# Four transformer blocks on one core: the boundaries between the stages, split finer and covered by one more row panel

## The reference

```python
h = x
for layer in range(2):
    y = rmsnorm(h, norm_g[layer, 0])
    y = gmlp_mixer(y, ...) if layer == 0 else diff_attention(y, ...)
    h = h + rmsnorm(y, norm_g[layer, 1])
    y = rmsnorm(h, norm_g[layer, 2])
    y = conv_ffn(y, ...)                 # (gelu(conv(y @ gate)) * conv(y @ up)) @ down, d_ff = 2816
    h = h + rmsnorm(y, norm_g[layer, 3])
x = h
x = x + 0.5 * swiglu(rms_norm(x, ffn1_norm), ...)
u = rms_norm(x, mix_norm) @ w_in
x = x + concat(mla_attention(u, ...), moba_attention(u, ...)) @ w_out
x = x + 0.5 * swiglu(rms_norm(x, ffn2_norm), ...)
return rms_norm(x, final_norm)
```

## Time and profile before

| | |
|---|---|
| median of three runs | 1125.63 us (1125.15 to 1126.83) |
| the profiled execution | 1125.67 us, span of its trace 1123.9 us |
| TensorE busy | 1079.8 us, 96% of the span |
| VectorE, ScalarE, GpSimd busy | 734.1, 606.5 and 37.8 us |
| granted TensorE clock, mean | 0.99 |

### The profile page before, as it was taken

How to read it: one execution, slowest core, us unless ns; L and a number is a source line. 1 busy time by engine, 2 the same in 40 slices (tenths; PEclk the granted TensorE clock), 3 DMA queues, 4 the chain that set the end, 5 groups by cost and what they waited for, 6 DMA issues and landing times.

```text
span 1123.9 us, 17895 instructions
## 1 busy us (share of the span) xinstructions
PE 1079.8 (96%) x7236; PEld 987.2 (88%) x7236; DVE 734.1 (65%) x1145; ACT 606.5 (54%) x1060; POOL 37.8 (3%) x39
## 2 busy tenths in 40 slices
PE   6999999999899789999999999999999989999997
PEld 4887999998799669999997999999899978999996
DVE  4887877666768667867667654455666846545543
ACT  5566665556655656655557543444455646344333
POOL 0640000000000000000000000000000000000000
PEclk9999999999999899999999999999999989999999
DMA  9664785565464225765563755555353514655541
GB/s 346 199 209 155 206 246 179 190 198 171 150 225 130 77 75 179 264 194 172 189 199 100 261 177 196 190 171 195 127 174 122 187 57 158 213 193 171 193 162 38
DMA packets 56257, 197.76 MB, mean 176 GB/s; under 512 B 6560, under 2 KB 8008, under 8 KB 56176
## 3 DMA queue, kind: packets, MB, share of 16 engines
q1 hardware_dynamic: 55920, 196.42, 53.8%
q0 software_dynamic: 112, 0.20, 0.1%
q10 hardware_dynamic: 144, 0.00, 0.0%
HBM read 195.35 MB, written 1.25 MB: 175 GB/s over the span
## 4 chain that ended last, share of the span: by engine, by line
PE 89%; DVE 5%; ACT 4%; issue 1%; DMA 0%; DVEq 0%; SPq 0%; ACTq 0%
PE Y L1260 25%; PE G L1225 16%; PE G L1227 16%; PE G L1226 16%; PE G L1248 3%; PE G L1249 3%; PE G L1250 3%; DVE w_low L744 1%; PE Y L1268 1%; PE Y L1226 1%; PE Y L1225 1%; PE Y L1227 1%; PE G L1378 1%; ACT big L431 1%; ACT L406 1%
## 5 line engine op out<-in xcount | busy, mean ns | idle before, releaser
L744 DVE TENSOR_TENSOR w_low<-raw,w_high 128x1024 fp32r<-128x1024 f32 x352 | 428.1, 1225 | 60.4 <-ACT w_high L399 59.0
L1225 PE MATMUL G<-x_parts,w_high 128*128 128x256 f32 x1504 | 426.6, 284 | 0.0
L1227 PE MATMUL G<-x_parts,w_low 128*128 128x256 f32 x1504 | 425.5, 283 | 0.0
L1226 PE MATMUL G<-x_parts,w_high 128*128 128x256 f32 x1504 | 425.5, 283 | 0.0
L399 ACT CAST w_high<-raw 128x1024 fp32r<-128x1024 f32 x352 | 359.5, 1046 | 11.5 <-DMA raw<-in_panels 7.8
L1225 PEld LDWEIGHTS G<-x_parts,w_high 128*128 128x128 f32 x1504 | 288.3, 192 | 3.4 <-DVE qk L875 0.3
L1226 PEld LDWEIGHTS G<-x_parts,w_high 128*128 128x128 f32 x1504 | 288.3, 192 | 2.7
L1227 PEld LDWEIGHTS G<-x_parts,w_low 128*128 128x128 f32 x1504 | 288.3, 192 | 0.0
L1260 PE MATMUL Y<-w_high,a_high 128*128 128x512 f32 x448 | 141.6, 398 | 3.9 <-DVE a_low L1057 2.0
L1260 PE MATMUL Y<-w_high,a_low 128*128 128x512 f32 x448 | 139.9, 393 | 0.0
L1260 PE MATMUL Y<-w_low,a_high 128*128 128x512 f32 x448 | 138.9, 391 | 0.0
(11 more groups left out here) (208 smaller groups left out, 935.2 us busy)
## 6 DMA issues: line engine op xcount, KB each, us to landing
raw<-in_panels SPq DMA_DIRECT2D x352, 512.0 KB, 4.5
gain_pre<-in_gains SPq DMA_DIRECT2D x7, 512.0 KB, 5.5
gain_post<-in_gains SPq DMA_DIRECT2D x4, 512.0 KB, 7.7
big<-in_xT SPq DMA_DIRECT2D x4, 256.0 KB, 8.0
h<-in_x SPq DMA_DIRECT2D x2, 512.0 KB, 8.7
big<-rel_rows SPq DMA_DIRECT2D x8, 128.0 KB, 6.1
out_y<-w SPq DMA_DIRECT2D x4, 256.0 KB, 2.0
big<-in_w_s SPq DMA_DIRECT2D x1, 512.0 KB, 10.1
```

The lines of the kernel that those rows point to most:

```text
L744: v.tensor_tensor(WL[:, n % RING, :], raw[:, n % RAWS, :], WH[:, n % RING, :].bitcast(F32), ALU.subtract).then_inc(lo, 1)
L1225: mm(out, WH[:, j, c:c + w], xh, start=first, stop=False, skip_group_check=skip)
L1226: mm(out, WH[:, j, c:c + w], xl, start=False, stop=False, skip_group_check=skip)
L1227: return mm(out, WL[:, j, c:c + w], xh, start=False, stop=last, skip_group_check=skip)
```

## The change

- `tail` takes the boundary's number and any number of row panels. The FFNs keep six row panels back for it instead of five (`_ffn_order`, `FFN_ORDER[4:-6]`); the two mixers' and the attention's tails keep five. `rows` for the last panel now goes by column halves: three matmuls for c = 0, then three for c = 1, each with its own signal (`y_there`).
- The transposes of the first token half's first four tiles are issued by `tail` itself: behind the last part (boundaries 1 and 3) or ahead of it (2, 4, 5 and 6: `early`).
- The normed stream, its transposes and its high and low parts are made in three pieces of 2, 2 and 4 tiles (`PARTS`) instead of two of 4; the third piece of t = 0 is turned into a bank of G. The transposes of t = 1 stand behind all matmuls of t = 0.
- The low parts of panels base + 3 and base + 4 are made by GpSimd (`BY_POOL`, `low_parts`), twelve panels in all; DVE leaves them out. ACT makes base + 4 within the boundary, before it reads the transposes.
- On DVE the gained copy of c = 0 comes first, and at boundaries 1 to 4 the third low part of t = 0 stands in the middle of the work on t = 1.
- Start: panel 6 is loaded ahead of x; ACT and DVE make panel 7 before the first and panel 8 before the second half of x's squares; PE computes the t = 1 products of panels 4 to 7 before it spreads the inverse roots (`r0_ps`), and DVE copies those (`rkvs`) after the first statistics instead of before them.
- End: `final_norm` multiplies h by the gain while ACT squares it, and scales one column half on ACT and the other on DVE.

```diff
+BY_POOL = [STARTS[b] + i for b in range(1, 7) for i in (3, 4)]
+PARTS = ((0, 2), (2, 2), (4, 4))
...
-        if 4 <= f < NF - 1:
+        if 4 <= f < NF - 2:
             seq.append(("d", f - 4))
-    return seq + [("d", f) for f in range(NF - 5, NF)]
+    return seq + [("d", f) for f in range(NF - 6, NF)]
...
# SyncE
-                    sp.wait_ge(lo, n - RAWS + 1)
+                    sp.wait_ge(*low_made(n - RAWS))
...
-            load(5)
+            load(5), load(6)
             for t in range(TT):
                 sp.dma_start(h[:, t, :], io["x"][t]).then_inc(x_in[t], 16)
-            load(6)
...
# GpSimd
+            def low_parts(b):
+                for n in BY_POOL[2 * (b - 1):2 * b]:
+                    pool.wait_ge(hi, n + 1)
+                    g.tensor_tensor(WL[:, n % RING, :], raw[:, n % RAWS, :], WH[:, n % RING, :].bitcast(F32),
+                                    ALU.subtract).then_inc(lo_pool, 1)
...
# ScalarE, boundary
                 if b in POST:
                     y_square(b, 0, 0), y_square(b, 0, 1)
                     y_root(b, 0)
                     upto(base + 3)
                 h_rms(b, 0)
-                if b < 7:
-                    x_high(b, 0, 0)
+                upto(base + 4)
+                x_high(b, 0, 0), x_high(b, 0, 1)
                 if b in POST:
                     y_square(b, 1, 0)
-                if b < 7:
-                    x_high(b, 0, 1)
+                x_high(b, 0, 2)
...
+            def final_norm():
+                for t in range(TT):
+                    h_rms(7, t)
+                    act.wait_ge(hg_r, 2 * t + 1)
+                    act.wait_ge(rs7_r, t + 1)
+                    s.activation(xn[:, t, half(0)], xn[:, t, half(0)], ACT.Copy, scale=rs2[:, t:t + 1])\
+                        .then_inc(out0_r, 1)
...
-            upto(6)
+            upto(7)
             h_rms(0, 0)
+            upto(8)
             h_rms(0, 1)
...
# VectorE, boundary
                 if b in POST:
-                    y_gained(b, 0, 1)
                     y_gained(b, 0, 0)
                     y_half_mean(b, 0)
+                    y_gained(b, 0, 1)
                     h_add(b, 0)
-                    half_mean(b, 0)
-                    upto(base + 3)
-                    x_normed(b, 0)
...
+                half_mean(b, 0)
+                x_normed(b, 0)
+                x_low(b, 0, 0), x_low(b, 0, 1)
+                if b in POST:
+                    y_gained(b, 1, 0)
+                    y_half_mean(b, 1)
+                    x_low(b, 0, 2)
+                    y_gained(b, 1, 1)
+                    h_add(b, 1)
                 else:
+                    x_low(b, 0, 2)
                     h_plus_y(b, 1)
...
+            def final_norm():
+                dve.wait_ge(gn_in, 16 * 7)
+                for t in range(TT):
+                    h_plus_y(7, t)
+                    dve.wait_ge(h_r, quarter(7, t, 1))
+                    for c in range(2):
+                        v.tensor_tensor(xn[:, t, half(c)], h[:, t, half(c)], gN[:, half(c)], ALU.mult).then_inc(hg_r, 1)
+                    half_mean(7, t)
+                    dve.wait_ge(h_std, 14 + t + 1)
+                    v.reciprocal(rs2[:, t:t + 1], sd2[:, t:t + 1]).then_inc(rs7_r, 1)
...
# TensorE, rows and tail
+                if last:
+                    for c in range(2):
+                        for x, w, start, stop in three:
+                            end = mm(Y[:, 2 * t + c, :], x, w[:, j, half(c)], start=start, stop=stop)
+                        end.then_inc(used if t == 1 and c == 1 else y_done, 1)
+                    return
...
-                for i in range(4):
+                for i in range(last):
                     part(i, 0)
                 part(0, 1)
-                part(4, 0).then_inc(y_done, 1)
-                for i in range(1, 4):
+                part(last, 0)
+                for i in range(1, last):
                     part(i, 1)
-                part(4, 1)
+                if early:
+                    turn_x(b, 0, 0), turn_x(b, 0, 1)
+                part(last, 1)
+                if b < 7:
+                    if not early:
+                        turn_x(b, 0, 0), turn_x(b, 0, 1)
+                    turn_x(b, 0, 2)
...
             value_panels(0, 4, (0,)).then_inc(v_ps, 1)
+            value_panels(0, 4, (1,))
             pe.wait_ge(rs0_r, 1)
...
             last.then_inc(r0_ps, 1)
-            value_panels(0, 4, (1,))
```

More of the change, by code:

```diff
@@ L251, in seen_turns, with low_made, y_there, sixth @@
             return a if a < HEADS else HEADS + 2 * (a - HEADS) + m
+        def low_made(n):
+            if n in BY_POOL:
+                return lo_pool, BY_POOL.index(n) + 1
+            return lo, n + 1 - sum(m < n for m in BY_POOL)
+        def y_there(b, t, c):
+            if t == 1 and c == 1:
+                return used, STARTS[b]
+            return y_done, 3 * (b - 1) + 2 * t + c + 1
+        def sixth(b, t, i):
+            return 6 * (b - 1) + 3 * t + i + 1
         def quarter(b, t, c):
@@ L381, in _ @@
             g.tensor_copy(bias[:, :, 0:P], bias[:, :, SC - P:SC]).then_inc(bias_r, 1)
+            for b in range(2, 6):
+                low_parts(b)
             pool.wait_ge(kr_r, 1)
@@ L436, in h_rms, with x_high @@
                     .then_inc(h_std, 1)
-            def x_high(b, t, c):
-                act.wait_ge(xt_r, quarter(b, t, c))
-                s.copy(x_half(0, t, c), y_half(t, c)).then_inc(xh_r, 1)
+            def x_high(b, t, i):
+                act.wait_ge(xt_r, sixth(b, t, i))
+                s.copy(x_rows(0, t, i), turned(t, i)).then_inc(xh_r, 1)
             def boundary(b, func):
@@ L730, in _ @@
             ffn(3, FFN3, False)
-            boundary(7, None)
+            final_norm()
         @block.vector
@@ L1212, in _ @@
             ffn(3, FFN3, False)
-            boundary(7)
+            final_norm()
         @block.tensor
@@ L1242, in values @@
                     if b:
-                        pe.wait_ge(xl_r, quarter(b, t, k // 4))
+                        pe.wait_ge(xl_r, sixth(b, t, min(k // 2, 2)))
                     else:
@@ L1257, in rows @@
                 xh, xl = AH[:, slot, tok(t)], AL[:, slot, tok(t)]
-                for x, w, start, stop in ((xh, WH, first, False), (xl, WH, False, False), (xh, WL, False, last)):
+                three = ((xh, WH, first, False), (xl, WH, False, False), (xh, WL, False, last))
+                if last:
[4 more added lines that the diff above has]
+                    return
+                for x, w, start, stop in three:
                     for c in range(2):
@@ L1300, in first_four @@
                     last.then_inc(done, 1)
-                turn_x(b, 1, 1)
+                for i in range(3):
+                    turn_x(b, 1, i)
                 for p in range(4):
@@ L1347, in ffn @@
                         tile_out(n, out(f, 0 if kind == "g" else 1))
-                last = range(NF - 5, NF)
-                tail(base + 3 * NF, [f % KT for f in last],
+                last = range(NF - 6, NF)
+                tail(b + 1, [f % KT for f in last], b < 6,
                      {(i, 0): (lambda f=f: hidden_seen(f)) for i, f in enumerate(last)})
@@ L1498, in _ @@
             head_rows(2, 1)
-            tail(FFN1, range(3, HEADS),
+            tail(3, range(3, HEADS), False,
                  {(0, 0): lambda: head_split(3),
@@ L1639, in _ @@
             weigh_values(15, 1)
-            tail(FFN3, [(k + 4) % KT for k in range(3, 8)],
+            tail(6, [(k + 4) % KT for k in range(3, 8)], True,
                  {(0, 0): lambda: out_split(3),
```

141 lines of the change are left out of this document (63 added, 78 removed).

## The result

The changed kernel took 1129.2 us (median of 11 runs, 1127.8 to 1133.2) against 1125.9 us for the kernel before in the same session: ratio 1.0025, 95% interval 1.0014 to 1.0035. So it is slower, by some 2.8 us, where 10.3 us of gain were forecast. Executions of one and the same kernel differ: the kernel before ran for 1125.1 to 1130.2 us, at mean granted clocks of 0.990 to 0.982, so a single trace shows one of several patterns of low clock.

The account below looks back on a forecast made before the run. TensorE, busy 1079.8 of 1123.9 us, was taken as the bound. Boundaries (2 x 1.35 + 0.3 + 1.8 + 0.85 + 0.75), start 4.3 and end 0.8 make 11.5, less 1.2 contention: 10.3 off 1125.7, 1115.4 us; range 1112.3 to 1119.8.

Parts of the forecast that it names:

- the contention: At the six boundaries, GpSimd's panels slow DVE by 0.2 us each, 1.2 us in all.
- (d): Rival: at boundaries GpSimd and DVE shut each other out on two SBUF inputs; up to 34 us, 1148 us; chance 0.05.
- twelve low panels ran beside GpSimd and eleven kept their time: Argument from the old trace's DVE rows against mutual shutting out: one low panel took 1.76 us instead of 1.22.
- GpSimd's own length: A 1024-column low panel takes GpSimd 2.8 us at the least, 7.1 at the most; its length costs nothing.
- The start: Before the first row sums: panel 7 ready earlier, so PE reaches them at 34.35 instead of 39.06; gain 4.3 us.
- Rival (b): At the start, late panel 7 or 9 or `rkvs` leaves only 1.3 of 4.3 us: 1118.4 us; chance 0.13.
- The boundaries: Earlier first t = 1 matmul: 1.35 us each at 1 and 3, 0.3 at 2, 1.8 at 4, 0.85 at 5, 0.75 at 6.
- rival (c): The clock stays up at boundary 2 and DVE is not disturbed: gain 12.7 us, 1113.0 us; chance 0.15.
- The wait of 2.8 us at boundary 2: PE waits 2.8 us before the first transposes, a clock drop is counted behind it, leaving 0.3 us gain.
- Rival (e): Split pieces and signals cost their savings; with another clock drop at boundary 4 and the start's loss, 1125 us; chance 0.03.
- In between PE runs through: Between the start, the boundaries and the end PE has no idle time, so no other edit can win there.
- The end: Behind the last matmul, the normed stream ends at E + 3.25 instead of E + 4.05, the store unchanged; gain 0.8 us.

Follow-up runs that it names:

- the fourth experiment: Changed kernel with GpSimd's two-input subtraction replaced by a one-input multiplication at the same places (result not the reference's): ratio 0.9904, 1115.1 us.
- the first experiment: Changed kernel with GpSimd's twelve low panels given back to DVE, all else kept: ratio 0.9907, 1115.4 us.
- the eighth experiment: Changed kernel with DVE making GpSimd's panels, lambdas' exponential behind boundary 2, final half mean between the gain multiplications, c = 1 stored first: ratio 0.9865, 1110.7 us.
- fifth: Changed kernel with each of GpSimd's twelve low panels made by four instructions of 256 columns instead of one of 1024: ratio 0.9938, 1118.9 us.
- ninth: Changed kernel with DVE's normed stream reading one SBUF input, the gain left out at boundaries 1 to 6 (another result): ratio 1.0028.
- tenth: Kernel of the eighth experiment with the first four tiles' transposes behind the last part at boundaries 2, 4, 5 and 6 too: ratio 0.9873, 1112.3 us.

## Why the prediction was wrong, point by point

**The step that failed** is the contention: "I take 0.2 a boundary, 1.2, near the median". The same kernel without GpSimd's panels (which by the prediction's estimate pays 0.2 a boundary on DVE instead) is 13.3 us faster, 12.6 by the spans. By the marks it is 3.7 us at boundary 1, 3.2, 3.8 and 2.6 at 2, 3 and 4, and 0.3 or less at 5 and 6, where four parts of PE cover it. At 1, 2 and 3 a part of it, 1.7 us each, is the low clock that only the kernel with the longer waits has. At 2 that part is not surely GpSimd's: in the fourth experiment the clock fell there behind a wait of 2.83 us, in the first it stayed up behind 3.04. It was mechanism (d) of the rivals, given 0.05: its threshold of 1.9 us a boundary was right (11.5 us of gains against 13 us over six, 2.1 to 2.2 each), its upper price, 5.6, was two panels laid fully into the chain.

**Why it was mis-sized.** The median of the earlier trace rows was read as a price, and the spread behind it as one outlier: "twelve low panels ran beside GpSimd and eleven kept their time". That is not what the trace of before holds. Five of the twelve took 1.41 to 1.76 us instead of 1.22, and the four that follow one another from 49.48 take 6.0 us where 4.9 would do:

```profile
49.48 6.01 DVE L744 TENSOR_TENSOR w_low<-raw,w_high 128x1024 fp32r<-128x1024 f32 x4
```

The lock itself was there to be seen as well. The first of four short DVE instructions with two SBUF inputs was issued at 65.46, just behind GpSimd's `dist<-dist,cst` (65.3, 1077 ns), and took three times as long as the others, until 0.29 us behind GpSimd's end:

```profile
L995 DVE TENSOR_TENSOR a_low<-big,a_high x4: 410/412/1233, 65.5 to 67.3; 128x256 fp32r<-128x256 f32 x4
```

The holds were small because what held was short or of the other kind: most of the GpSimd instructions beside DVE's low panels were one-input TENSOR_SCALARs, which hold little (the fourth experiment), and the two-input ones had 128 to 384 columns and took 0.5 to 1.1 us where nothing held them. GpSimd's own row of 1.77 us for work that took 0.73 elsewhere was a hold too, seen from the other side. A hold grows with the instruction that holds: beside 1024 columns a DVE instruction took up to 2.2 us longer, beside quarters up to 0.55.

**GpSimd's own length**: 2.8 us "at the least" was forecast, 2.34 to 2.97 measured, and nobody waited for its result. Right but for the least, and of no importance: what mattered was beside whom it ran, not who waited for it.

**The start**: 4.3 forecast, 3.8 measured behind `rkvs` and the offsets, which are late by 0.25 and 0.33 us. The same start gave 3.5 alone, and 3.0 to 4.3 in the other traces that have it. Rival (b) did not come.

**The boundaries**, from the last row of the table: 1.7 at boundary 1 against 1.35 less 0.2; at 2, 1.3 against 0.3, because the clock stayed up there, which was rival (c)'s half (in the fourth experiment it fell at the same place); 1.6 at 3 against 1.35 less 0.2; 1.5 at 4 against 1.8 less 0.2; 0.8 at 5 against 0.85; 0.3 at 6 against 0.75. The wait of 2.8 us at boundary 2 came as 3.0. So the reckoning of the boundaries was sound. That the sum without GpSimd (11.5 less 1.2 for DVE's panels, 1115.4) is just what the first experiment measured is partly luck: more came at boundaries 1 to 3, less at the start, at 6 and at the end, and the low stretch between 5 and 6 took 1.5 that no term had. Rival (e)'s 1125 does not follow from the prices given for it: 1.65 us of clock and the 3.0 of (b) are 4.65 of 11.5.

**"In between PE runs through"** was a wrong reading, and the profile's summary ahead of the prediction has it too. Of PE's idle time in the kernel before some 8 us stand between 370 and 400, inside the second mixer, and 3 at 907 in the attention mixer, about as much as at boundaries 1 to 6 together (12 us):

```profile
372.49 0.49 PE L1390 MATMUL G<-big,w 128*128 128x128 f32 x2 [2.85 <-ACT w L530]
...
907.08 0.82 PE L1378 MATMUL G<-cst,w 128*128 128x128 f32 x3 [2.55 <-ACT w L524]
```

The change did not touch them, so the forecast does not hang on it, but "no other edit can win there" was not shown.

**The end**: 0.8 forecast, none measured. The last result came at 3.5 us behind the last matmul instead of 3.25, because DVE takes `half_mean` behind both multiplications and the root waits for it:

```profile
1121.27 1.29 DVE L860 TENSOR_TENSOR w<-h,gain_pre 128x512 f32<-128x512 f32 x2
...
1122.48 0.15 DVE L812 TENSOR_SCALAR bt<-ss 128x1 f32<-128x1 f32 x1
1122.72 0.29 ACT L466 ACTIVATE sd<-ss,bt 128x1 f32<-128x1 f32 x1 [0.73 <-DVE bt L812]
```

and the end of the span comes 3.1 us behind the last result instead of 2.5. Two stores are now issued at once, which may be why; in the eighth experiment, with c = 1 first, it was still 2.9. "The store behind it stays" was the wrong sentence.

**What stays open.** Three low stretches of the clock around 372 instead of two, and one between boundaries 5 and 6, come in most kernels with the new order and also, at 372, with the start alone; the fifth, ninth and tenth experiments have the new order and none between 5 and 6, the tenth two around 370. The one between 5 and 6 is worth 1.5 us; the third around 372 costs nothing against the kernel before, presumably because PE waits there for other engines anyway. What brings them is not settled: each kernel has one trace, and executions of one kernel differ in their mean clock.

## What to carry to other kernels

Before work is given to an idle GpSimd, list DVE's instructions that will run beside it by where their operands lie. Here those with an operand in PSUM ran free, and so did those of one column; the wide ones with everything in SBUF, where GpSimd read two inputs, stood until its instruction ended, up to 2.2 us each for instructions of 2.4 us. If such work must go there, put it where DVE waits anyway, cut it into short instructions, or find a one-input form; and when a trace of before is to price it, take only rows with the same kinds of operands on both sides, and look at every one of them, since a median of twelve hid five that were held.

## What the runs showed of the hardware that was not expected

- DVE and GpSimd hold each other by the instruction: a DVE piece of 0.48 us took up to 2.56, one of 0.75 up to 2.93, and a GpSimd quarter of 744 ns up to 1307.
- A one-input DVE instruction from SBUF to SBUF is held as well (3.83 us for three pieces beside GpSimd).
- GpSimd's one-input form on 1024 columns is longer than its two-input form (2.77 against 2.34 us where nothing held them, up to 3.35 against 2.97 where something did), and yet the kernel took 13.6 us less with it.
